# The first expert's token rows gathered as columns: products of x blocks with the place matrix, instead of a gather, a copy and a transpose

## The chip, the cores and the metric

One NeuronCore of one Trainium2 chip runs the whole kernel. The time is device time of one execution, in microseconds (us). All data are float32. Matrix products run on TensorE (PE in the profile; its weight loads are a row of their own, PEld), elementwise work on VectorE (DVE) and ScalarE (ACT), a few constants on GpSimd (POOL), and nearly all loads from HBM are issued by SyncE (SP).

## The reference, cut to what matters

One decoder layer over 256 tokens of width 1024: a mixer, then a mixture of experts. Only the second part is touched.

```python
x = x + hybrid_mixer(rmsnorm(x, g_mix), ...)
h = rmsnorm(x, g_ffn)
x = x + moe(h, ...)          # top 4 of 32 experts
out = rmsnorm(x, g_final)

# moe, per expert e, for the tokens that chose it:
logits = h @ w_router + b_router
top_v, top_i = lax.top_k(logits, 4)
gates = softmax(top_v)
gu = xb @ w_gate_up[e] + b_gate_up[e]
glu = min(gu[:, :F], 7) * sigmoid(1.702 * min(gu[:, :F], 7))
out_e = ((clip(gu[:, F:], -7, 7) + 1) * glu) @ w_down[e] + b_down[e]
```

## The kernel before

**The mixer** runs first, to about 133 us: projections, the gated linear attention, the output projection (`out_project`, L1352), all in 128x128 weight blocks.

**The experts** follow as 32 items, one for each expert, with 64 token slots each. An item's weights are six chunks of 2 MB (`gate_up` uses chunks 0 to 3, `down` chunks 4 and 5), which go through a ring of 12 slots in SBUF. SP issues the load of a chunk when the chunk that held its slot has been used (`s_used`; for the first chunk of item 0 also by quarters, `s_quarter`, and for some others by halves, `s_half`). For items 4 to 27 SP issues chunks in pairs of 4 MB (L457), when both slots of the pair are free; the first of these waits on item 2.

**An item's tokens** are found by a place matrix. `p_row[token, slot]` is 1/rms of the token where the token has this slot of the expert, else 0. `p_gate` is the same with the gate in place of 1/rms, over 128 columns. `gather` (L1389) multiplies `p_row` as 64 columns of weights with the residual stream `xs` (`x_sb` in the profile), 512 columns at a time, so that `bank[3]` holds the 64 gathered rows, one half of the width in partitions 0 to 63 and the other in 64 to 127. ACT copies this to `x_row`, TensorE transposes it in blocks of 128 (`turn_gathered`), and DVE scales it by the norm's weight into `x_t` (`keep_turned`), whose blocks `x_t[:, k, :]` are the weights in `gate_up`. For item `it + 1` this happens under the products of item `it`. For item 0 nothing lies ahead of it but the router, so it is written out by hand.

**From the residual stream to item 0**, the stretch of the change, PE's order is: the last part of `out_project`; logits of the second token tile, blocks 4 and 5 (`logits(1, 4, 6)`); the transposes of x blocks 6 and 7 (`transpose_x(1, 6, 8, 5)`, L1361), which wait for DVE's last addition to `xs` (L960); two idle products (`idle`, L1339, on constants); logits of blocks 6 and 7, which wait for DVE's copy of the transposes (L996, `s_trD`); a product that starts the second tile's ranks (L1427); the gather of tile 0; the rank product of tile 1 (L1431), which waits for DVE's choice of the experts (`chosen`, L964 to L969); the counts (L1433); one idle product; the gather of tile 1, which waits for the second `p_row` (L975); two idle products; `turn_first`: the transposes of the gathered rows in two halves (L1453), each when ACT has copied its half (L690), with an idle product between them, and then two transposes of `gates4` (L1458); then item 0's first product, which waits for DVE's first half of `x_t` (L1038, `s_xt_a`). Under the gather DVE turns the logits into gates (L1003 to L1009, with one exponential on ACT), copies them four times side by side (`gates4`, L1033), and scales the two halves of `x_t` (L1038). After them it writes item 0's `p_gate` (L1021) and waits for the transposed gates (`s_gt`), which it keeps as `gates_t` (L1044).

**Inside item 0** (`products`), PE runs chunk 0 (16 matmul records in the trace, two for each float32 product), the two transposes of `p_gate` (`turn_gates`, L1547), chunk 1, and so on. ACT's first copy into the second half of `gu_sb` waits for `s_gt`.

Of the kernel before, what the change touches and what calls it, by code (L numbers as in the profile page):

```python
# [6 lines left out]
P = 128  # L7
D = 1024
T = 256
TT = T // P  # L10
KT = D // P
# [18 lines left out]
SLOTS = 64  # L30
# [121 lines left out]
def build(nc, x, x_cols, cols_in, w_in, w_gk_down, w_gk_up, w_out, w_router, b_router, w_expert, b_gate_up, w_down_last, b_down, norm_final_g, out):  # L152
# [3 lines left out]
    ALU = mybir.AluOpType  # L156
# [8 lines left out]
    with ctx:  # L165
        def sem(name):
            return ctx.enter_context(nc.semaphore(name))
# [191 lines left out]
        s_xg = sem("x_gathered")  # L359
        s_xr_a = sem("first_x_row_half_ready")  # L360
        s_xT_a = sem("first_x_half_turned")
# [227 lines left out]
        def _(act_e):  # L589
# [97 lines left out]

            for f in range(2):
                act_e.wait_ge(s_xg, 1)
                act_e.copy(x_row[:, f * 256:(f + 1) * 256], bank[3][:, f * 256:(f + 1) * 256]).then_inc((s_xr_a, s_xr)[f], 1)  # L690
            act_e.preload_act_table_set("sigmoid_and_others")

            def keep_gathered(it):

                act_e.wait_ge(s_xg, it + 1)
                act_e.copy(x_row[:, :], bank[3][:, :]).then_inc(s_xr, 1)  # L696
# [99 lines left out]
        def _(dve):  # L796
            steps = [0]

            def link(ins):
                steps[0] += 1  # L800
                ins.then_inc(s_dve, 1)
                dve.wait_ge(s_dve, steps[0])
# [168 lines left out]
            def rank_and_place(t):  # L971
# [34 lines left out]
            link(dve.tensor_tensor(ex[:, :, :], ex[:, :, :], chosen[:, :, :], ALU.mult))  # L1006
            link(dve.tensor_reduce(ngt[:, :], ex[:, :, :], AX.X, ALU.add))
            link(dve.reciprocal(ngt[:, :], ngt[:, :]))
            dve.tensor_tensor(gates[:, :, :], ex[:, :, :],  # L1009
                              ngt[:, :].rearrange("p (t a) -> p t a", a=1).broadcast_to([P, TT, E]), ALU.mult).then_inc(s_gtk, 1)  # L1010
            dve.wait_ge(s_gtk, 1)

            def place_rows(e, slots):
# [11 lines left out]
            def keep_turned(it):  # L1025
# [8 lines left out]
                            .broadcast_to([P, TT, SPLITS, E])).then_inc(s_gtk, 1)  # L1034
            for i in range(2):
                dve.wait_ge((s_xT_a, s_xT)[i], 1)
                f = slice(2 * i, 2 * i + 2)
                dve.tensor_tensor(x_t[:, :, :].rearrange("p (a f) s -> p a f s", a=2)[:, :, f, :],  # L1038
                                  bank[(2, 4)[i]][:, 0:256].rearrange("p (f a s) -> p a f s", f=2, a=2),
                                  cols[:, COL_FFN:COL_FFN + KT].rearrange("p (a f s) -> p a f s", a=2, s=1)[:, :, f, :]  # L1040
                                  .broadcast_to([P, 2, 2, SLOTS]), ALU.mult).then_inc((s_xt_a, s_xt)[i], 1)
            place_gates(0, slot1[:, :])
# [138 lines left out]
        def _(pe):  # L1181
# [154 lines left out]
            def idle(n):  # L1336

                for _ in range(n):
                    mm(bank[1][:, 0:P], ones[:, :], before[:, :], start=True, stop=True)  # L1339
# [45 lines left out]
            def gather(ts=range(TT)):  # L1385
# [5 lines left out]
                if TT - 1 in ts:  # L1391
                    ins.then_inc(s_xg, 1)

            every = range(KT)
            out_project(0, 0, 0, every, False)
# [24 lines left out]
            pe.wait_ge(s_trA, 4)  # L1420
            logits(1, 4, 6)
            transpose_x(1, 6, 8, 5)
            idle(2)
            pe.wait_ge(s_trD, 1)
            logits(1, 6, 8)
            pe.wait_ge(s_p0, 1)
            mm(bank[5][:, E:2 * E], ones[:, :], chosen[:, 0, :], start=True, stop=False)  # L1427
            gather([0])

# [6 lines left out]
            pe.wait_ge(s_p0, 2)  # L1436
            gather([1])
            idle(2)
            nb = BLOCKS - 1

            def turn_gathered(it):

                pe.wait_ge(s_xr, it + 1)
                for f in range(4):
                    ins = nc.tensor.transpose(bank[3][:, f * P:(f + 1) * P], x_row[:, f * P:(f + 1) * P], ident[:, :])  # L1445
                ins.then_inc(s_xT, 1)

            def turn_first():

                for i in range(2):  # L1450
                    pe.wait_ge((s_xr_a, s_xr)[i], 1)
                    for f in range(2 * i, 2 * i + 2):
                        ins = nc.tensor.transpose(bank[(2, 4)[i]][:, f % 2 * P:(f % 2 + 1) * P], x_row[:, f * P:(f + 1) * P], ident[:, :])  # L1453
                    ins.then_inc((s_xT_a, s_xT)[i], 1)
                    idle(1 - i)
                pe.wait_ge(s_gtk, 2)
                for t in range(TT):
                    ins = nc.tensor.transpose(bank[6][:, t * P:(t + 1) * P],  # L1458
                                              gates4[:, t, :, :].rearrange("p a e -> p (a e)"), ident[:, :])
                ins.then_inc(s_gt, 1)  # L1460

            turn_first()

# [25 lines left out]
            def gate_up(it, j, ks):  # L1489
# [6 lines left out]
                for kk in ks:  # L1496
                    if in_pieces and kk % 2 == 0:
                        pe.wait_ge(s_piece[it, j][kk // 2], 16)
                    k = 4 * (j % 2) + kk
                    if isinstance(it, int) and it == 0 and k == 2:  # L1500
                        pe.wait_ge(s_xt, 1)
# [67 lines left out]
            def products(it, following):  # L1569
# [5 lines left out]
                gate_up(it, 0, range(4))  # L1575
                turn_gates(it)
                gate_up(it, 1, range(4))
                if known == 1:
# [180 lines left out]
```

## Time and profile before

| what | value |
|---|---|
| median of 3 runs | 1042.41 us (1041.95 to 1043.14) |
| the profiled execution, its own time | 1042.84 us |
| its span in the trace | 1041.1 us |
| PE busy | 1009.0 us (97%) |
| chain that ended last | PE 79%, DMA 19%, issue 1% |
| HBM read | 422.48 MB, 407 GB/s over the span |
| item 0's products begin | 139.95 us |

Times in the rows are microseconds from the start of the span. A float32 product shows as two weight loads and two matmuls (x2), a transpose as one of each. The ends of matmuls are modelled, so the profile's rows of PE overlap by some tenths of a microsecond, and the rows of PEld, whose starts are apart by what a load occupies, say more exactly when PE took the next piece of work.

### The profile page before, as it was taken

To read this page: it belongs to the slowest core of one execution; us is meant where nothing else is said; L and a number is where in the kernel's file an instruction comes from. 1 tells how busy PE (TensorE), PEld (TensorE's weight loads), DVE (VectorE), ACT (ScalarE), POOL (GpSimd) and SP (SyncE) were. 2 spreads that over 40 slices of the span, in tenths; PEclk is the share of its full clock that TensorE was granted. 3 is DMA by queue.
4 is the path that set the end of the run, shared out by engine and by line. 5 is a ranking of instruction groups with operands and counts; after the bars stand their busy time and mean duration, and the time that the engine had idled before them with its cause. 6 is when DMAs were issued, how large, how long until landed. Compare 5 with 4: busy or idle time off the path is not lost.

```text
span 1041.1 us, 12117 instructions
## 1 busy us (share of the span) xinstructions
PE 1009.0 (97%) x4824; PEld 412.3 (40%) x4824; DVE 245.0 (24%) x625; ACT 140.8 (14%) x281; POOL 6.5 (1%) x24
## 2 busy tenths in 40 slices
PE   8999999999999999999999999999999999999996
PEld 7688843333333333333333333333333333333333
DVE  2264132112122222222221122221212121122122
ACT  1100121111111111111111111111111111111112
POOL 1000000000000000000000000000000000000000
PEclk9999999999999999999999999999999999999999
DMA  9983789999999999999999999999999999999995
GB/s 367 408 369 134 311 343 422 387 426 423 420 435 429 429 434 429 434 429 434 429 428 436 431 433 429 429 434 429 436 428 434 429 428 436 426 427 427 426 421 222
DMA packets 23270, 423.86 MB, mean 407 GB/s; under 512 B 2888, under 2 KB 3408, under 8 KB 5840
## 3 DMA queue, kind: packets, MB, share of 16 engines
q1 hardware_dynamic: 22320, 422.45, 95.6%
q10 hardware_dynamic: 928, 1.09, 0.3%
q8 instruction: 17, 0.28, 0.1%
q14 instruction: 5, 0.04, 0.0%
HBM read 422.48 MB, written 1.05 MB: 407 GB/s over the span
## 4 chain that ended last, share of the span: by engine, by line
PE 79%; DMA 19%; issue 1%; DVE 0%; ACT 0%; SPq 0%; DVEq 0%; PEldq 0%
PE bank L1503 33%; DMA ring<-in_w_expert 19%; PE bank L1523 18%; PE bank L1243 5%; PE bank L1389 5%; PE y L1566 4%; PE bank L1541 3%; PE y L1352 2%; PE bank L1227 1%; PE bank L1445 1%; PE bank L1218 1%; PE bank L1352 1%; PE bank L1547 1%; PE bank L1624 1%; DMA h_t<-in_x_cols 1%
## 5 line engine op out<-in xcount | busy, mean ns | idle before, releaser
L1503 PE MATMUL bank<-ring,x_t 128*64 128x512 f32 x1984 | 447.1, 597 | 0.0
L1523 PE MATMUL bank<-ring,act 128*64 128x512 f32 x992 | 230.5, 596 | 14.2 <-DMA ring<-in_w_expert 14.2
L1503 PEld LDWEIGHTS bank<-ring,x_t 128*64 128x64 f32 x1984 | 133.9, 136 | 261.9 <-issue 257.1
L1523 PEld LDWEIGHTS bank<-ring,act 128*64 128x64 f32 x992 | 68.4, 137 | 145.2 <-issue 144.5
L1076 DVE TENSOR_TENSOR gu_b<-bank,bias_t 128x512 f32<-128x512 f32 x64 | 44.2, 691 | 330.3 <-PE bank L1541 330.2
L704 ACT COPY gu_sb<-bank 128x512 f32<-128x512 f32 x64 | 37.4, 585 | 222.6 <-PE bank L1503 222.6
L1566 PE MATMUL y<-z,p_t 64*128 64x512 f32 x248 | 61.6, 615 | 0.0
L1389 PE MATMUL bank<-x_sb,p_row 128*64 128x512 f32 x256 | 60.6, 593 | 0.0
L1029 DVE TENSOR_TENSOR x_t<-bank,cols 128x512 f32<-128x512 f32 x30 | 20.7, 691 | 164.9 <-PE bank L1445 164.9
L1243 PE MATMUL bank<-h_t,ring 128*128 128x256 f32 x256 | 56.1, 380 | 0.0
L1015 DVE TENSOR_SCALAR p_row<-slot,rank,rstd 128x64 f32<-128x64 f32 x62 | 16.7, 311 | 165.1 <-PE bank L1547 165.1
L708 ACT ACTIVATE act<-gu_b 128x256 f32<-128x256 f32 x62 | 25.8, 416 | 196.0 <-DVE gu_b L1082 196.0
L1243 PEld LDWEIGHTS bank<-h_t,ring 128*128 128x128 f32 x256 | 48.4, 190 | 7.0 <-issue 0.5
L1541 PEld LDWEIGHTS bank<-ident,gu_sb 128*128 128x128 f32 x256 | 26.8, 140 | 50.7 <-issue 50.2
L1541 PE MATMUL bank<-ident,gu_sb 128*128 128x128 f32 x256 | 42.0, 286 | 0.1
L700 ACT COPY p_t<-bank 128x256 f32<-128x256 f32 x31 | 11.5, 372 | 189.6 <-PE bank L1547 189.6
L1389 PEld LDWEIGHTS bank<-x_sb,p_row 128*64 128x64 f32 x256 | 18.2, 137 | 35.6 <-issue 35.4
L712 ACT COPY z<-bank 128x512 f32<-128x512 f32 x31 | 18.2, 587 | 89.3 <-PE bank L1523 89.3
L1566 PEld LDWEIGHTS y<-z,p_t 64*128 64x128 f32 x248 | 21.3, 186 | 20.0 <-issue 15.0
L1092 DVE TENSOR_TENSOR act<-act,gu_b 128x256 f32<-128x256 f32 x62 | 26.3, 425 | 6.5
L1087 DVE SCALAR_TENSOR_TENSOR gu_b<-gu_b 128x256 f32<-128x256 f32 x64 | 27.2, 425 | 2.2
L696 ACT COPY x_row<-bank 128x512 f32<-128x512 f32 x31 | 18.1, 585 | 62.8 <-PE bank L1389 62.8
(231 smaller groups left out, 403.2 us busy)
## 6 DMA issues: line engine op xcount, KB each, us to landing
ring<-in_w_expert SPq DMA_DIRECT2D x72, 4096.0 KB, 36.1
ring<-in_w_expert SPq DMA_DIRECT2D x36, 2048.0 KB, 47.4
ring<-in_w_expert SPq DMA_DIRECT2D x18, 1024.0 KB, 10.7
ring<-in_w_in SPq DMA_DIRECT2D x5, 2048.0 KB, 25.1
ring<-in_w_out SPq DMA_DIRECT2D x2, 2048.0 KB, 26.9
ring<-in_w_expert SPq DMA_DIRECT2D x4, 512.0 KB, 5.6
ring<-in_w_down_last SPq DMA_DIRECT2D x4, 512.0 KB, 25.3
ring<-in_w_down_last SPq DMA_DIRECT2D x2, 1024.0 KB, 24.6
```

The source lines that it names most:

```text
L704: act_e.copy(gu_sb[:, h, :], bank[h][:, :]).then_inc(s_guk, 1)
L708: act_e.activation(act_of(it)[:, 4 * h:4 * h + 4, :], gu_b[:, 0, :, :], ACT.Sigmoid, scale=ALPHA).then_inc(s_sig, 1)
L1076: dve.tensor_tensor(gu_b[:, :, :, :], bank[2][:, :].rearrange("p (f a s) -> p a f s", a=2, f=4), bias_t[:, :, 4 * h:4 * h + 4, ds(e, 1)] . ...
L1087: dve.scalar_tensor_tensor(out=gu_b[:, 1, :, :], in0=gu_b[:, 1, :, :], scalar=1.0, in1=gu_b[:, 0, :, :], op0=ALU.add, op1=ALU.mult).then_i ...
L1092: dve.tensor_tensor(act_of(it)[:, 4 * h:4 * h + 4, :], act_of(it)[:, 4 * h:4 * h + 4, :], gu_b[:, 1, :, :], ALU.mult).then_inc(s_av, 1)
L1243: ins = mm(dst[:, m * T:(m + 1) * T], w[:, k, (2 * i + m) * P:(2 * i + m + 1) * P], h_t[:, k, :], start=k == 0, stop=k == KT - 1)
L1352: ins = mm(dst[:, c0:c0 + 256], y_t[:, k, t * P:(t + 1) * P], w[:, k, :], start=j == 0, stop=j == KT - 1)
L1389: ins = mm(bank[3][a * SLOTS:(a + 1) * SLOTS, :], p_row[:, t, :], xs[:, t, a * HALF:(a + 1) * HALF], start=t == 0, stop=t == TT - 1)
L1503: ins = mm(bank[h][a * SLOTS:(a + 1) * SLOTS, :], x_t_of(it)[:, k, :], w[:, kk, a, :], start=k == 0, stop=k == KT - 1)
L1523: ins = mm(bank[0][a * SLOTS:(a + 1) * SLOTS, :], act_of(it)[:, k, :], w[:, kk, a, :], start=k == 0, stop=k == KT - 1)
L1541: ins = nc.tensor.transpose(bank[2][:, f * P:(f + 1) * P], gu_sb[:, h, f * P:(f + 1) * P], ident[:, :])
L1566: mm(y_ps[t][nn][:, :], p_t_of(it)[r, t * P:(t + 1) * P], z[r, :], start=first, stop=False, skip_group_check=True).then_inc(s_y, 1)
```

## The change

Item 0's rows are gathered the other way round. `gather_first` takes a 128x128 block of `xs` as the weights and `p_row` as the 64 moving columns, eight blocks for each of the two token tiles. The result is already turned: four blocks in `bank[2]`, four in `bank[3]`. So ACT's two copies to `x_row`, the four transposes behind them, and five of the six idle products go. DVE's two scalings (`keep_first`) read the two banks, blocks 0 to 3 and blocks 4 to 7, and stand further ahead in DVE's order. The eight products of tile 0 are spread over three places: two ahead of the last transposes of x, three in place of two idle products, three in place of the gather of tile 0. The two transposes of `gates4` move behind item 0's first chunk (`turn_all_gates`). Item 0 waits for the second half of `x_t` at its fourth block instead of its third.

```diff
-            for f in range(2):
-                act_e.wait_ge(s_xg, 1)
-                act_e.copy(x_row[:, f * 256:(f + 1) * 256], bank[3][:, f * 256:(f + 1) * 256]).then_inc((s_xr_a, s_xr)[f], 1)
...
             link(dve.tensor_reduce(ngt[:, :], ex[:, :, :], AX.X, ALU.add))
+
+            def keep_first(i):
+
+                dve.wait_ge((s_xT_a, s_xT)[i], 1)
+                k = slice(i * KT // 2, (i + 1) * KT // 2)
+                dve.tensor_tensor(x_t[:, k, :], bank[2 + i][:, 0:KT // 2 * SLOTS].rearrange("p (k s) -> p k s", s=SLOTS),
+                                  cols[:, COL_FFN:COL_FFN + KT].rearrange("p (k s) -> p k s", s=1)[:, k, :]
+                                  .broadcast_to([P, KT // 2, SLOTS]), ALU.mult).then_inc((s_xt_a, s_xt)[i], 1)
+
+            keep_first(0)
             link(dve.reciprocal(ngt[:, :], ngt[:, :]))
...
             dve.wait_ge(s_gtk, 1)
+            keep_first(1)
...
-            for i in range(2):
-                dve.wait_ge((s_xT_a, s_xT)[i], 1)
-                f = slice(2 * i, 2 * i + 2)
-                dve.tensor_tensor(x_t[:, :, :].rearrange("p (a f) s -> p a f s", a=2)[:, :, f, :],
...
+            def gather_first(t, k0, k1):
+
+                for k in range(k0, k1):
+                    f = k % (KT // 2)
+                    ins = mm(bank[2 + k // (KT // 2)][:, f * SLOTS:(f + 1) * SLOTS], xs[:, t, k * P:(k + 1) * P], p_row[:, t, :],
+                             start=t == 0 and f == 0, stop=t == TT - 1 and f == KT // 2 - 1, skip_group_check=True)
+                    if t == TT - 1 and f == KT // 2 - 1:
+                        ins.then_inc((s_xT_a, s_xT)[k // (KT // 2)], 1)
...
             logits(1, 4, 6)
+            pe.wait_ge(s_p0, 1)
+            gather_first(0, 0, 2)
             transpose_x(1, 6, 8, 5)
-            idle(2)
+            gather_first(0, 2, 5)
             pe.wait_ge(s_trD, 1)
             logits(1, 6, 8)
-            pe.wait_ge(s_p0, 1)
             mm(bank[5][:, E:2 * E], ones[:, :], chosen[:, 0, :], start=True, stop=False)
-            gather([0])
+            gather_first(0, 5, KT)
...
             idle(1)
             pe.wait_ge(s_p0, 2)
-            gather([1])
-            idle(2)
+            gather_first(1, 0, KT)
...
-            def turn_first():
-
-                for i in range(2):
-                    pe.wait_ge((s_xr_a, s_xr)[i], 1)
-                    for f in range(2 * i, 2 * i + 2):
-                        ins = nc.tensor.transpose(bank[(2, 4)[i]][:, f % 2 * P:(f % 2 + 1) * P], x_row[:, f * P:(f + 1) * P], ident[:, :])
-                    ins.then_inc((s_xT_a, s_xT)[i], 1)
-                    idle(1 - i)
+            def turn_all_gates():
                 pe.wait_ge(s_gtk, 2)
                 for t in range(TT):
...
-                    if isinstance(it, int) and it == 0 and k == 2:
+                    if isinstance(it, int) and it == 0 and k == 3:
                         pe.wait_ge(s_xt, 1)
...
                 turn_gates(it)
+                if known == 0:
+                    turn_all_gates()
                 gate_up(it, 1, range(4))
```

How the order of work moves is shown on two engines. On PE, from the logits of the second tile (`logits`, L1367) to the end of item 0's second chunk, the kernel before has these rows (a row's `x2` counts products here, not passes; `out<-moving,weights`):

```order
L1367 MATMUL y<-wr_g,h_t 128x32 x2
L1361 MATMUL y<-ident,x_sb 128x128 x2
L1339 MATMUL bank<-before,ones 128x128 x2
L1367 MATMUL y<-wr_g,h_t 128x32 x2
L1427 MATMUL y<-chosen,ones 128x32
L1389 MATMUL bank<-x_sb,p_row 64x512 x2
L1431 MATMUL y<-chosen,before 128x32
L1433 MATMUL y<-ones,chosen 32x1 x2
L1339 MATMUL bank<-before,ones 128x128
L1389 MATMUL bank<-x_sb,p_row 64x512 x2
L1339 MATMUL bank<-before,ones 128x128 x2
L1453 MATMUL bank<-ident,x_row 128x128 x2
```

Between the last of these and item 0's chunk 0 (L1503) stand one more idle product, the other two transposes of `x_row` and the two transposes of the gates (L1458).

The same stretch of PE in the changed kernel, where L1398 is `gather_first` and L1460 the transposes of the gates:

```order
L1367 MATMUL y<-wr_g,h_t 128x32 x2
L1398 MATMUL bank<-p_row,x_sb 128x64 x2
L1361 MATMUL y<-ident,x_sb 128x128 x2
L1398 MATMUL bank<-p_row,x_sb 128x64 x3
L1367 MATMUL y<-wr_g,h_t 128x32 x2
L1437 MATMUL y<-chosen,ones 128x32
L1398 MATMUL bank<-p_row,x_sb 128x64 x3
L1441 MATMUL y<-chosen,before 128x32
L1443 MATMUL y<-ones,chosen 32x1 x2
L1339 MATMUL bank<-before,ones 128x128
L1398 MATMUL bank<-p_row,x_sb 128x64 x8
L1503 MATMUL bank<-ring_49,x_t 64x512 x8
```

The row `x8` of L1503, item 0's chunk 0, now stands directly behind the last gather. The two transposes of the gates follow one row later, behind those of `p_gate`.

On DVE, from the end of the second `p_row` to item 0's `p_gate`, the kernel before has:

```order
L1003 TENSOR_TENSOR ex<-lg,lmax 128x64
L1006 TENSOR_TENSOR ex<-ex,chosen 128x64
L1007 TENSOR_REDUCE ngt<-ex 128x2
L1008 RECIPROCAL ngt<-ngt 128x2
L1009 TENSOR_TENSOR gates<-ex,ngt 128x64
L1033 COPY gates_63<-gates 128x256
L1038 TENSOR_TENSOR x_t<-bank,cols 128x2x128
L1038 TENSOR_TENSOR x_t<-y,cols 128x2x128
L1021 TENSOR_SCALAR p_gate<-slot_73,rank_75,gates 128x128 x2
```

The same stretch of DVE in the changed kernel, with `keep_first` as L1009 and the gates as L1015, has:

```order
L999 TENSOR_TENSOR ex<-lg,lmax 128x64
L1002 TENSOR_TENSOR ex<-ex,chosen 128x64
L1003 TENSOR_REDUCE ngt<-ex 128x2
L1009 TENSOR_TENSOR x_t<-bank,cols 128x256
L1014 RECIPROCAL ngt<-ngt 128x2
L1015 TENSOR_TENSOR gates<-ex,ngt 128x64
L1009 TENSOR_TENSOR x_t<-bank,cols 128x256
L1040 COPY gates_63<-gates 128x256
L1028 TENSOR_SCALAR p_gate<-slot_73,rank_75,gates 128x128 x2
```

The first half of `x_t` has moved ahead of the reciprocal and the gates, the second ahead of the copy of the gates.

## Rows read from the trace of the kernel before

**Rows 1.** The page, busy time of each engine (share of the span) and instructions.

```profile
PE 1009.0 (97%) x4824; PEld 412.3 (40%) x4824; DVE 245.0 (24%) x625; ACT 140.8 (14%) x281; POOL 6.5 (1%) x24
```

**Rows 2.** Chain that ended last, from 600 us: start, us, what.

```profile
683.45 3.46 PE bank L1523 x16
...
687.28 48.20 DMA ring<-in_w_expert
```

**Rows 3.** Who waited for whom: us in total, times, longest.

```profile
SPq L457 <- PE bank L1503: 397.9, 48, 10.7
...
PE bank L1523 <- DMA ring<-in_w_expert: 14.2, 8, 1.8
```

**Rows 4.** Windows: PE, PEld, DVE, ACT, POOL busy; granted clock, DMA share, GB/s.

```profile
150.00:200.00 50.00, 49.68 (x232) 16.80 (x228) 11.90 (x36) 6.14 (x12) 0.00 (x0) 1.00 1.01 424
...
204.00:205.00 1.00, 1.00 (x16) 0.53 (x16) 0.16 (x1) 0.54 (x1) 0.00 (x0) 1.00 0.08 33
...
210.00:250.00 40.00, 39.84 (x188) 13.50 (x186) 7.85 (x20) 5.14 (x10) 0.00 (x0) 1.00 1.01 427
```

**Rows 5.** Chain that ended last, from 115 to 145 us.

```profile
133.38 0.45 PE y L1361 x2
...
133.85 0.44 DVE h_t L996
...
134.34 0.65 PE y L1367 x4
...
136.33 0.41 PE y L1431 x2
...
137.37 1.08 PE bank L1389 x4
...
139.80 0.22 PE y L1458 x2
140.02 3.58 PE bank L1503 x16
143.60 0.37 PE bank L1547 x2
```

**Rows 6.** Weight loads in order of time: start, their time together, line, xcount.

```profile
127.96 0.97 PEld L1367 LDWEIGHTS y<-wr_g,h_t 128*128 128x128 f32 x8 [0.64 <-ACT h_t L661]
...
132.42 0.63 PEld L1367 LDWEIGHTS y<-wr_g,h_t 128*128 128x128 f32 x4
133.38 0.20 PEld L1361 LDWEIGHTS y<-ident,x_sb 128*128 128x128 f32 x2 [0.33 <-DVE x_sb L960]
133.55 0.53 PEld L1339 LDWEIGHTS bank<-before,ones 128*128 128x128 f32 x4
134.33 0.52 PEld L1367 LDWEIGHTS y<-wr_g,h_t 128*128 128x128 f32 x4 [0.26 <-DVE h_t L996]
134.78 0.30 PEld L1427 LDWEIGHTS y<-chosen,ones 128*128 128x128 f32 x2
135.12 0.20 PEld L1389 LDWEIGHTS bank<-x_sb,p_row 128*64 128x64 f32 x4
```

**Rows 7.** DVE in order of time, 138 to 150 us.

```profile
138.09 0.22 DVE L1007 TENSOR_REDUCE ngt<-ex 128x2 f32<-128x64 f32 x1
...
139.40 0.42 DVE L1038 TENSOR_TENSOR x_t<-bank,cols 128x256 f32<-128x256 f32 x1 [0.30 <-PE bank L1453]
...
149.90 0.69 DVE L1076 TENSOR_TENSOR gu_b<-bank,bias_t 128x512 f32<-128x512 f32 x1 [4.76 <-PE bank L1541]
```

**Rows 8.** PE in order of time, 66 to 72 us: start, time together, line, xcount.

```profile
69.71 1.56 PE L1321 MATMUL y<-q_dec,state 64*128 64x64 f32 x24
```

**Rows 9.** Weight loads in order of time, 80 to 150 us, columns as in Rows 6.

```profile
100.43 13.79 PEld L1352 LDWEIGHTS y<-ring,y_t 128*128 128x128 f32 x64
```

**Rows 10.** One window in the kernel's last microseconds, columns as in Rows 4.

```profile
1036.00:1038.00 2.00, 0.00 (x0) 0.00 (x0) 1.06 (x3) 0.86 (x1) 0.00 (x0) 0.50 0.36 132
```

**Rows 11.** The last products on PE, in order of time, 1028 to 1041 us.

```profile
1031.88 1.14 PE L1633 MATMUL y<-z,p_t_last 64*128 64x256 f32 x8 [0.56 <-ACT z L758]
```

More of the change, by code:

```diff
@@ L359, in build @@
         s_xg = sem("x_gathered")
-        s_xr_a = sem("first_x_row_half_ready")
         s_xT_a = sem("first_x_half_turned")
@@ L685, in _ @@
             act_e.activation(ex[:, :, :], ex[:, :, :], ACT.Exp).then_inc(s_le, 1)
-            for f in range(2):
-                act_e.wait_ge(s_xg, 1)
-                act_e.copy(x_row[:, f * 256:(f + 1) * 256], bank[3][:, f * 256:(f + 1) * 256]).then_inc((s_xr_a, s_xr)[f], 1)
             act_e.preload_act_table_set("sigmoid_and_others")
             def keep_gathered(it):
-                act_e.wait_ge(s_xg, it + 1)
+                act_e.wait_ge(s_xg, it)
                 act_e.copy(x_row[:, :], bank[3][:, :]).then_inc(s_xr, 1)
@@ L1034, in _ @@
                             .broadcast_to([P, TT, SPLITS, E])).then_inc(s_gtk, 1)
-            for i in range(2):
-                dve.wait_ge((s_xT_a, s_xT)[i], 1)
-                f = slice(2 * i, 2 * i + 2)
-                dve.tensor_tensor(x_t[:, :, :].rearrange("p (a f) s -> p a f s", a=2)[:, :, f, :],
-                                  bank[(2, 4)[i]][:, 0:256].rearrange("p (f a s) -> p a f s", f=2, a=2),
-                                  cols[:, COL_FFN:COL_FFN + KT].rearrange("p (a f s) -> p a f s", a=2, s=1)[:, :, f, :]
-                                  .broadcast_to([P, 2, 2, SLOTS]), ALU.mult).then_inc((s_xt_a, s_xt)[i], 1)
             place_gates(0, slot1[:, :])
@@ L1436, in _ @@
             pe.wait_ge(s_p0, 2)
-            gather([1])
-            idle(2)
+            gather_first(1, 0, KT)
             nb = BLOCKS - 1
             def turn_gathered(it):
-                pe.wait_ge(s_xr, it + 1)
+                pe.wait_ge(s_xr, it)
                 for f in range(4):
@@ L1460, in turn_first @@
                 ins.then_inc(s_gt, 1)
-            turn_first()
             def count_extras():
```

## The prediction, made before the changed kernel ran

> **What bounds the kernel now.** I read the page first: PE is busy 97% of the span [rows 1]. That is a busy share, not yet a bound, so the chain of waits comes next. From item 0 to 687 us the chain is PE's own work without a break. Then it turns: a chunk pair comes free, SP issues its load at once, the load lands 48.20 us later and PE waited for it [rows 2]. The list of waits says the same: SP waited 48 times on products, 397.9 us in all, and PE waited 8 times for weights, 14.2 us in all [rows 3]. So late in the loop the weight stream ends last; it moves some 430 GB/s without a pause.
>
> What starts that stream? The windows show the DMA engines full from 150 to 200 us, all but empty at 204 to 205 us (share 0.08), and full again from 210 us [rows 4]. At 204 us they wait for PE: the first pair load of the loop needs two chunks of item 2 to be used. PE itself is never late there (busy 49.68 of 50 us). The stream therefore starts at a moment that PE sets, with nothing left over from before. A microsecond that PE gains or loses before item 0 reaches 204 us whole, and from there the end, one for one. Thus the sum is made on PE's path from 132 to 144 us.
>
> In that stretch the chain is [rows 5]: DVE's last addition to x, two transposes of it, DVE's copy (over at 134.29), the logits, DVE's choice, the rank product at 136.33, the second gather at 137.37, then ACT's copy, the transposes, the gates' transposes, and item 0's 16 matmuls, over at 143.60.
>
> **The price of one new product.** It has 128x128 weights and 64 moving columns, in two passes. No row has exactly this. Two rows bracket it: logits (32 moving columns) and idle products (128 moving columns). Eight loads of the first take 0.97 us with the last alone 0.19, so (0.97 - 0.19)/7 = 0.111 us apart; four of the second (0.53 - 0.19)/3 = 0.113 [rows 6]. Narrower and wider cost the same, so the load sets the pace and 64 columns should too: 0.222 us a product. The far bounds are 0.13 (24 passes of 64x64 in 1.56 us [rows 8], half the rows, half the columns) and 0.43 (64 loads at 256 columns in 13.79 us [rows 9]). I take 0.222.
>
> The Trainium skill ("TensorE: Matmul & The Clock Gate", Back-to-back issue gap) gives about 81 ns for each matmul in a sustained stream of load and matmul at 128 columns, which would be 0.16 us a product. The rows here have 0.111 us a pass where it has 0.081. By the page the eight last products would take 1.30 us instead of 1.78 and the gain would be some 0.4 us larger; the sum goes by the rows.
>
> **Part by part.**
>
> 1. *Two products ahead of the last transposes.* The loads of the logits begin at 132.42 and take 0.63 us, the last of them 0.19, so the next could begin at 132.42 + 0.63 - 0.19 + 0.11 = 132.97. DVE releases the transposes at 133.38. The four new loads take 132.97 to 133.41 [rows 6]. The gap holds them but for 0.03 us; since the matmuls behind them have to drain too, I take a delay of 0.05 (0 to 0.2). Everything on the chain down to the second gather shifts with it. `p_row` of tile 0, for which they wait, is long there. If the products cost more, there is no cover here: each 0.1 us a product is 0.2 us.
>
> 2. *Three products for two idle ones.* Six loads, 0.67 us, from 133.60 end at 134.27; DVE's copy ends at 134.29 + 0.05. Cost 0, with 0.07 us to spare; at a higher price the logits wait.
>
> 3. *Three products for the gather of tile 0.* The old gather ran 1.08 us from 135.12, hidden ahead of the rank product at 136.33 [rows 5]. The new ones load from about 135.06 to 135.72 and end near 136.0. Hidden, 0.3 us to spare.
>
> 4. *Tile 1.* Begins at 137.37 + 0.05 = 137.42. Sixteen loads, 0.111 apart: the last begins at 139.09. Meanwhile the first half: its last load begins at 138.20, its product ends 0.3 later (logits: last load 134.66, end 134.99), 138.5; DVE is free since 138.31 + 0.05 [rows 7]; scaling 0.42 us, and some 0.1 to wake PE: 139.05. So the first half of `x_t` is ready just before PE has finished the second half of the gather, and PE binds, by 0.1 to 0.2 us. Item 0's first load follows the last one by 0.11 or, as 64-column loads behind 128-column ones do (134.89 to 135.12 [rows 6]), by 0.23: 139.32. Before, it was 139.95. So chunk 0 starts and ends 0.63 us earlier. The second half of `x_t` is scaled behind the gates by about 139.95, and is needed at the fourth block, 6 x 0.224 us after 139.32, which is 140.66: hidden, 0.7 to spare.
>
> 5. *Out of the way:* ACT's copies, four transposes, three idle products, the gates' transposes and their waits are what made up 138.45 to 139.95 [rows 5, 6]; they are replaced, not added, and already counted in 4. ACT's table load moves ahead and nobody waits for it.
>
> 6. *The gates' transposes behind chunk 0.* On the chain the two took 0.22 us before item 0 [rows 5]; now they take 0.22 us behind `p_gate`'s. Their gates are ready by about 140.3, chunk 0 ends near 143.0. What waits behind them: chunk 1, 0.22 us later; on DVE the copy of the gates, the counts and item 1's places, some 2 us of work from about 143.6, when its next work that is waited for begins at 149.90 [rows 7]; on ACT the second half of gate and up, some 10 us later. All hidden.
>
> 7. *SP.* No issue moves in its order. The quarters of chunk 0 come free 0.6 us earlier, while the DMA engines have some slack; that fills a gap that 204 us forgets anyway.
>
> **Sum:** +0.05 (already in the 0.63) - 0.63 + 0.22 = -0.41 us at chunk 1, and the same at the end. The profiled execution, 1042.84 us, would become 1042.43; the median of the runs shown is 0.43 below it, 1042.41, so about **1042.0 us**.
>
> About 0.2% (2.1 us) is what a measurement of this kernel can tell from no change, and the three runs shown are themselves 1.2 us apart. The forecast is inside that.
>
> **The rivals.**
>
> *The new products cost 0.43 us each (slower).* A float32 weight load from `xs` behind narrow products could run at the pace of the wide ones [rows 9]. Then parts 1 and 2 delay the logits by 0.42 + 0.6 = 1.0, tile 1 takes 3.4 us instead of 1.78, and item 0 begins near 141.9: +1.9, plus 0.22, gives 1044.5. It turns from gain to loss at (13 products on the path, 0.41 us to lose) 0.222 + 0.03 = 0.25 us a product. Against it: both rows of Rows 6 with 0.11 us a pass. For it: the turning point is near.
>
> *The clock falls (slower).* Idle products and wide gathers are replaced by narrow products. The one low window is in the last microseconds, 0.50 from 1036 us on [rows 10], after PE had stopped at 1033.02 [rows 11]. Against it: PE stands still for 3 us there and nowhere here, and the change opens no new gap on it. If half the clock held for some 4 us of item 0, it would cost 2 us: 1044.0.
>
> *No effect at the end.* If the stream were bound before 204 us, the gain would be lost: 1042.4. Against it: the empty window [rows 4].
>
> *The first half of `x_t` binds after all.* If its semaphore and DVE's read of PSUM take 0.3 us more than in part 4, PE waits for it: gain 0.2, 1042.2. That margin is only 0.1 to 0.2 us.
>
> *Cheaper products (faster).* At 0.13 [rows 8] tile 1's products take 1.0 us, and DVE's first scaling binds: free at 138.36, done at 138.8, PE at 138.9. Item 0 begins 1.05 us earlier, less 0.22: gain 0.8, 1041.6. (The page's 0.16 us, above, would fall under this rival.)
>
> **Chances.** Forecast (gain 0.3 to 0.6) 0.54; the half of `x_t` binds 0.08; no effect 0.12; cheaper products 0.12; dearer products 0.06; clock 0.04; something unseen, either side, 0.04. The range has to hold the middle cases and the scatter of a median of a few such runs (those shown lie 0.5 below and 0.7 above theirs), and reaches some way to the dear ones: 1040.9 to 1043.5. By more than 0.2%: faster 0.03, slower 0.05, within 0.92.
>
> **What would show it.** PE's loads of L1398 0.111 us apart; the last transposes of x (L1361) at 133.38 to 133.5; the second `p_row` at most 0.1 later; item 0's first load at 139.2 to 139.5; `p_gate`'s transposes 0.6 and chunk 1 0.4 earlier; the first pair load of the loop at 204.2 instead of 204.6. It would be wrong if L1398's loads stand further apart than 0.125, if PE waits for `x_t`, if the windows from 132 to 150 show a clock below 1.00, or if the 0.4 us at 204 us is not there at 687 us.

## The result: slower by 2.5 us, because TensorE's clock falls to half ahead of item 0 and in it

The changed kernel took 1045.28 us (median of 16 runs, 1044.15 to 1046.13) against 1042.78 us of the kernel before (16 runs, 1041.95 to 1043.37). The ratio is 1.0023, with a 95% interval of 1.0016 to 1.0029. The forecast was 1042.0 us, with a range up to 1043.5. The profiled execution took 1044.50 us, span 1042.7 us (before: 1042.84 and 1041.1). One more execution of the kernel before, beside the first experiments, was in a slow state at 2673.49 us and is left out of every count below.

The first place to look is item 0's chunk 0, since the forecast's sum ends there. This is the chain of waits of the changed kernel from 115 to 145 us (start, us, what), to be read against [rows 5]:

```profile
132.58 0.36 PE y L1367 x4
132.95 0.47 PE bank L1398 x4
133.42 0.23 PE y L1361 x2
133.65 0.62 PE bank L1398 x6
134.26 0.55 PE y L1367 x4
...
136.16 0.41 PE y L1441 x2
...
137.20 2.37 PE bank L1398 x16
139.57 4.84 PE bank L1503 x16
144.41 0.37 PE bank L1547 x2
144.78 0.22 PE y L1460 x2
```

L1398 is `gather_first`. Up to 137.20 all went by the forecast. Then the 16 matmuls of tile 1's gather take 2.37 us, where they take 2.00 in the same code with the clock kept (e6 below), and the same 16 matmuls of chunk 0 that took 3.58 us before take 4.84. Nothing waits there. The windows of the same kernel say why (us, then PE, PEld, DVE, ACT, POOL busy; **granted clock**, DMA share, GB/s):

```profile
130.00:136.00 6.00, 5.71 (x41) 5.20 (x40) 2.31 (x11) 1.38 (x5) 0.00 (x0) 1.00 0.61 224
136.00:137.00 1.00, 0.84 (x8) 0.79 (x8) 0.46 (x3) 0.00 (x0) 0.00 (x0) 1.00 1.20 492
137.00:138.00 1.00, 1.00 (x9) 0.81 (x9) 0.59 (x4) 0.62 (x2) 0.00 (x0) 1.00 1.15 492
138.00:139.00 1.00, 1.00 (x10) 1.00 (x9) 0.69 (x4) 0.92 (x1) 0.00 (x0) 0.83 0.69 295
139.00:140.00 1.00, 1.00 (x5) 0.67 (x6) 0.49 (x2) 0.00 (x0) 0.00 (x0) 0.50 1.22 524
140.00:141.00 1.00, 1.00 (x4) 0.24 (x2) 0.81 (x4) 0.00 (x0) 0.00 (x0) 0.50 1.07 459
141.00:142.00 1.00, 1.00 (x4) 0.24 (x2) 0.00 (x0) 0.00 (x0) 0.00 (x0) 0.50 0.22 82
142.00:143.00 1.00, 1.00 (x8) 0.32 (x6) 0.00 (x0) 0.00 (x0) 0.00 (x0) 0.96 0.64 66
```

The granted clock is 1.00 until 138.7, 0.50 (1.2 of 2.4 GHz) until 142.1, then 1.00 again. PE is busy the whole time that it is low, with half as many matmuls in a window (x4 for x8). Before the change it was 1.00 from the first product to the last, and PE was no busier ahead of 138 us than after it. Windows of the kernel before:

```profile
130.00:136.00 6.00, 5.71 (x34) 4.33 (x33) 2.17 (x10) 1.38 (x5) 0.00 (x0) 1.00 0.63 229
136.00:137.00 1.00, 0.87 (x9) 0.62 (x8) 0.43 (x3) 0.00 (x0) 0.00 (x0) 1.00 1.29 541
```

From 130 to 138 us PE stands idle for 0.42 us in the kernel before and for 0.45 in the changed one. What differs is what it does: the windows count 49 matmuls before and 58 after. The mean granted clock shows it in every run: 0.994 to 0.996 in all 16 runs of the changed kernel, 0.997 or 0.998 in the kernel before, where only the end, after PE's last product [rows 10, 11], is low.

The page after, to [rows 1]: PE has ten matmuls more (32 for 16 new products, less 8 of the old gather, 10 of idle products and 4 transposes), and 1.7 us more busy time, about what the stretch at half clock adds (0.37 and 1.26 us):

```profile
PE 1010.7 (97%) x4834; PEld 414.7 (40%) x4834; DVE 244.8 (23%) x625; ACT 140.2 (13%) x279; POOL 6.5 (1%) x24
```

### The profile page after: what moved, and what is told of

It reads as the page before. It is cut to its first block, busy times and chain, and to the rows that moved or that the text cites. A ratio compares the mean times of both kernels' runs of the same rounds, so it can differ in the third digit from the quotient of the medians.

```text
span 1042.7 us, 12111 instructions
## 1 busy us (share of the span) xinstructions
PE 1010.7 (97%) x4834; PEld 414.7 (40%) x4834; DVE 244.8 (23%) x625; ACT 140.2 (13%) x279; POOL 6.5 (1%) x24
## 4 chain that ended last, share of the span: by engine, by line
PE 75%; DMA 23%; issue 1%; DVE 0%; ACT 0%; SPq 0%; DVEq 0%; PEldq 0%
PE bank L1503 30%; DMA ring<-in_w_expert 23%; PE bank L1523 18%; PE bank L1243 5%; PE bank L1389 4%; PE y L1566 4%; PE bank L1541 3%; PE y L1352 2%; PE bank L1227 1%; PE bank L1454 1%; PE bank L1218 1%; PE bank L1352 1%; PE bank L1547 1%; PE bank L1626 1%; DMA h_t<-in_x_cols 1%
## 5 line engine op out<-in xcount | busy, mean ns | idle before, releaser
L1503 PE MATMUL bank<-ring,x_t 128*64 128x512 f32 x1984 | 448.3, 598 | 0.0
L1503 PEld LDWEIGHTS bank<-ring,x_t 128*64 128x64 f32 x1984 | 134.2, 137 | 262.8 <-issue 257.9
L1389 PE MATMUL bank<-x_sb,p_row 128*64 128x512 f32 x248 | 58.5, 592 | 0.0
```

What stands on the lines that cost most here:

```text
L1389: ins = mm(bank[3][a * SLOTS:(a + 1) * SLOTS, :], p_row[:, t, :], xs[:, t, a * HALF:(a + 1) * HALF], start=t == 0, stop=t == TT - 1)
L1503: ins = mm(bank[h][a * SLOTS:(a + 1) * SLOTS, :], x_t_of(it)[:, k, :], w[:, kk, a, :], start=k == 0, stop=k == KT - 1)
```

## The experiments

Two theories stood at the start. **The clock:** with the new gather PE has less of the work that keeps the clock up, and the loss is the spell at half clock. **The rival:** the loss comes from the order (the gates' transposes behind chunk 0, DVE's copies ahead), and the clock is a side show.

The kernels ran in three sets (e1 to e4, e5 to e8, e9 to e12), each on one chip with the kernel before (medians 1042.96, 1042.97 and 1043.10 us). To compare profiles, I count from the end of the output projection in the chain (132.81 us in the kernel before), which executions reach up to 0.6 us apart.

| kernel | median against before, us | ratio, 95% interval | runs with mean clock 0.996 or less | to chunk 0, us | to chunk 1, us |
|---|---|---|---|---|---|
| before | | | 0 of 94 | 7.21 | 11.16 |
| changed | +2.50 | 1.0016 to 1.0029 | 16 of 16 | 6.99 | 12.42 |
| e1_gates_only | +0.06 | 0.9992 to 1.0010 | 0 of 11 | 7.06 | 11.30 |
| e2_wide_fill | +0.07 | 0.9992 to 1.0010 | 0 of 11 | 7.19 | 11.36 |
| e3_128_columns | -0.37 | 0.9988 to 1.0005 | 0 of 11 | 6.71 | 10.88 |
| e4_no_idle | -0.07 | 0.9999 to 1.0016 | 4 of 12 | 7.07 | 11.09 |
| e5_changed_again | +2.00 | 1.0009 to 1.0027 | 10 of 11 | 8.50 | 13.67 |
| e6_two_idle_back | -0.54 | 0.9985 to 1.0004 | 0 of 11 | 6.62 | 10.79 |
| e7_gates_ahead | +3.83 | 1.0025 to 1.0052 | 5 of 5 | 8.60 | 14.63 |
| e8_128_tile0 | -0.46 | 0.9994 to 1.0012 | 3 of 11 | 6.66 | 10.83 |
| e9_128_tile1 | +1.00 | 1.0001 to 1.0019 | 6 of 11 | 7.93 | 12.10 |
| e10_128_and_idle | -0.49 | 0.9987 to 1.0005 | 0 of 11 | 6.71 | 10.88 |
| e11_idle_gates_ahead | +0.82 | 1.0000 to 1.0019 | 2 of 11 | 7.83 | 11.78 |
| e12_two_idle_again | -0.87 | 0.9984 to 1.0002 | 0 of 11 | 6.61 | 10.78 |

The last two columns are of the profiled execution alone, the others of all runs. Where a kernel keeps its clock in one run and loses it in another, the profile shows one case only: one that kept it in e4, e8 and e11, one that lost it in e5 and e9. The interval goes by the means of the runs, so the few long runs of e4 and e8 lift it above what the median says. The mean clock of a run is rounded to 0.001, which is some 2 us at half clock, so a spell of up to about 2 us can hide in a 0.997: the counts of runs that fell are lower bounds.

### One part alone: the gates' transposes

```diff
--- before
+            def turn_all_gates():      # the last lines of turn_first, now a function of their own
...
                 turn_gates(it)
+                if known == 0:
+                    turn_all_gates()
                 gate_up(it, 1, range(4))
```

> The kernel before with one part of the change alone: the two transposes of the gates stand behind item 0's first chunk. Theory (the loss is the clock that falls to half at 138.7 us, and narrow products in the gather bring it): here the gather is the old one, so the granted clock stays 1.00 from 130 to 150 us, item 0 starts 0.2 us earlier and its second chunk at the same time; the median is that of the kernel before within 0.3 us. Rival (what is put behind the first chunk makes the wait, on DVE or ACT): the loss of some 2 us appears here too.

Measured: 1043.02 against 1042.96 us, with the clock at 1.00 from 130 to 150 us in the profile. On the old gather this part costs nothing, so the rival falls as far as one part alone can show it (with the new gather: e7 and e11). It gains nothing either, since chunk 0 now waits for DVE's first half of `x_t` where it stood behind the transposes.

### More columns in PE's gaps

```diff
--- changed
             gather_first(0, 5, KT)
+            wide(1)        # ones x xs[:, 0, 0:512] into bank[1]
...
-            idle(1)
+            wide(1)
```

> The changed kernel with one product of 512 moving columns in the gap ahead of the rank product of tile 1, and another in place of the idle product of 128 columns behind the counts. Both should fit into time in which PE waits for DVE (0.58 us and 0.42 us). Theory (what PE streamed ahead of 138.7 us lets the clock fall): with more columns streamed the granted clock stays 1.00, chunk 0 takes 3.6 instead of 4.84 us, and the median comes to 0.4 us below the kernel before. Rival (the clock falls whatever fills the gaps, or the loss has another source): 1045 us again.

Measured: 1043.03 against 1042.96 us; the clock is 1.00 in the windows from 130 to 150 us and chunk 0 takes 3.58 us. The clock theory holds, but the gain is gone too. The chain of this kernel (L1406 is the wide product, L1447 the rank product):

```profile
136.20 0.91 PE bank L1406 x2
137.12 0.14 PE y L1447 x2
...
137.47 1.06 PE bank L1406 x2
138.53 1.73 PE bank L1398 x16
140.26 3.58 PE bank L1509 x16
```

The two did not fit into the gaps; they hold 0.91 and 1.06 us of the chain, and tile 1's gather starts 5.46 us behind the output projection, against 4.62 in e6 below. My expectation had them fit into waits of 0.58 and 0.42 us.

### 128 moving columns instead of 64

The cut is shortened; DVE's scaling, not shown, reads the first 64 of every 128 columns.

```diff
--- changed
-   mm(bank[..][:, f * SLOTS:(f + 1) * SLOTS], xs[..], p_row[:, t, :], ...)
+   mm(bank[..][:, f * P:(f + 1) * P], xs[..],
+      p_row[:, t, :].rearrange("p (a s) -> p a s", a=1).broadcast_to([P, 2, SLOTS]), ...)
```

> The changed kernel with each gathering product streaming its 64 place columns twice, so 128 moving columns; the second copy goes to columns of PSUM that nobody reads. The weight loads set the pace (0.111 us a pass at 32 and at 128 columns), so PE's times should not change. Theory (narrow products bring the clock down): the clock stays at 1.00 or falls for less, and the median is 1042.4 to 1043.5. Rival (not the columns but the weight loads, the order or the gap ahead of the rank product): the clock falls as before, 1045 us.

Measured: 1042.59 against 1042.96 us, mean clock 0.997 or 0.998 in all 11 runs. The same number of products in the same order, the same wait of 0.58 us ahead of the rank product, and little time added (chunk 0 at 6.71 us, against 6.62 in e6):

```profile
137.84 2.05 PE bank L1398 x16
139.89 3.58 PE bank L1504 x16
```

Tile 1's products take 2.05 us here and 2.00 in e6 with 64 columns. So the order of the work, the weight loads and the wait are not enough to let the clock fall. How wide the products are makes the difference, for 0.09 us.

### The kernel before without its idle products

```diff
--- before
-            idle(2)        # and idle(1), idle(2), idle(1 - i): six products in all
```

> The kernel before without its six idle products (L1339), all else as it was. If idle products hold the clock up in this stretch, it falls to half between 135 and 143 us here too, although the wide gathers are there: +1.5 to +2.5 us. If the wide gathers are enough, the clock stays 1.00 and the median is 0 to 0.5 us below that of the kernel before.

Measured: a median of 1042.89 us, but in two groups. Eight of 12 runs took 1041.76 to 1043.67 us at a mean clock of 0.997 or 0.998, and four took 1043.91 to 1046.15 at 0.994 or 0.995. Neither expectation is met alone. The wide gathers mostly hold the clock by themselves, but not always, and with the idle products the kernel before never lost it in 94 runs. So they were not filler that could go for free, which is how the forecast counted them. The profile caught a run that held the clock, with PE idle for longer than in the changed kernel:

```profile
130.00:136.00 6.00, 5.26 (x31) 4.02 (x30) 1.96 (x8) 1.38 (x5) 0.00 (x0) 1.00 0.63 231
136.00:138.00 2.00, 1.45 (x10) 0.69 (x10) 1.08 (x6) 0.25 (x1) 0.00 (x0) 1.00 1.13 471
```

That is 1.29 us of idle time in 8, against 0.45 in the changed kernel, which lost the clock in 26 of its 27 runs (the first 16 and e5). PE's idle time alone does not decide it.

### The changed kernel again, profiled in its slower group

> The changed kernel once more, beside the next three on one chip. Its 16 runs so far lie in two groups: 1044.2 to 1044.5 with a mean granted clock of 0.996, and 1044.9 to 1046.1 with 0.994. Theory: in the first the half clock holds once for 3.4 us from about 138.7, in the second for about twice that, which (1 - 0.994) - (1 - 0.996) of 1043 us at half clock, 4 us, would be. A profile from the second group would show the low clock reach to 145 us and item 0's second chunk slowed too. Rival: the second group has its low clock elsewhere, or the weight stream takes longer there.

Measured: 1044.97 us. Six of the 11 runs are at 0.994, two at 0.995, two at 0.996 (1043.16 and 1044.10) and one at 0.998 (1043.24). The profile fell into the slower group. Windows of it, columns as above:

```profile
136.00:136.50 0.50, 0.12 (x2) 0.00 (x0) 0.44 (x3) 0.00 (x0) 0.00 (x0) 1.00 1.12 475
136.50:137.00 0.50, 0.44 (x2) 0.44 (x2) 0.01 (x1) 0.00 (x0) 0.00 (x0) 0.64 1.15 475
137.00:137.50 0.50, 0.50 (x6) 0.42 (x6) 0.28 (x2) 0.00 (x0) 0.00 (x0) 0.50 0.94 377
...
143.00:143.50 0.50, 0.50 (x4) 0.24 (x2) 0.00 (x0) 0.00 (x0) 0.00 (x0) 0.53 0.08 33
143.50:144.00 0.50, 0.50 (x4) 0.14 (x2) 0.00 (x0) 0.00 (x0) 0.00 (x0) 1.00 0.00 0
```

and its chain:

```profile
138.18 3.31 PE bank L1398 x16
141.49 4.58 PE bank L1503 x16
146.07 0.37 PE bank L1547 x2
```

The half clock lasts from 136.6 to 143.5, some 6.8 us where the other profile has 3.4. It slows tile 1's gather (3.31 for 2.00 us) and chunk 0 (4.58 for 3.58). Chunk 1 begins 2.5 us later than in the kernel before, where the other profile lost 1.26. That the two groups of times are these two lengths is what the two profiles and the mean clocks fit; my expectation put the second spell's end at 145 us, 1.5 too late, and chunk 1 was not slowed.

### Two idle products back

```diff
--- changed
             gather_first(0, 5, KT)
+            idle(2)
 
             pe.wait_ge(s_cho, 2)
```

> The changed kernel with two idle products of 128 columns in the gap ahead of the rank product of tile 1, where PE waited 0.58 us. If the clock falls because PE stood still there, it stays at 1.00 now and the median is 0.3 us below the kernel before. If what counts is how much PE streams over the whole stretch, 512 columns are a small part and the clock falls as before in most runs: 1044 to 1046 us.

Measured: 1042.43 against 1042.97 us, clock 0.997 or 0.998 in all 11 runs. That is the first case of the expectation: the wait is filled and the clock stays. It does not prove that the wait was the cause, since the two products also add columns, and since e3 holds the clock with the wait left as it was. The chain:

```profile
135.50 0.70 PE bank L1398 x6
136.19 0.50 PE bank L1339 x4
136.69 0.35 PE y L1442 x2
...
137.68 2.00 PE bank L1398 x16
139.68 3.58 PE bank L1504 x16
...
143.85 5.30 PE bank L1504 x24
```

The idle products fill the time in which PE waited for DVE's choice, and the rank product starts 3.63 us behind the output projection, 0.06 later than in e5.

> The changed kernel with two idle products back in the gap, a second time, to see its gain over the kernel before on one more set of runs: 0.4 us by the prediction's sum (the first set gave 0.54), with the clock at 1.00 in every run until PE stops.

Measured on a second set of runs: 1042.23 against 1043.10 us, clock 0.997 or 0.998 in all 11. Twice the changed kernel with two more idle products is ahead of the kernel before, by 0.54 and 0.87 us, each time with an interval that still includes 1.

### The gates ahead of item 0, at the low and at the full clock

```diff
--- changed (e7), and with idle(2) back (e11)
+            turn_all_gates()
...
-                if known == 0:
-                    turn_all_gates()
```

> The changed kernel with the other part undone: the gates' transposes stand ahead of item 0 again. By the theory (the narrow products bring the clock down) it loses as the changed kernel does: 1044 to 1046 us, mean granted clock 0.994 to 0.996. Rival (the second part of the change is the cause): 1042.6.

Measured: 1046.80 us, 3.83 over the kernel before, all five runs at 0.993 to 0.995. The loss is there without the second part of the change, as the theory has it, and is larger by 1.8 us than in e5. In the two profiles chunk 1 is 0.96 us later (14.63 against 13.67). The full clock shows where that comes from:

> The two idle products back, and the gates' transposes ahead of item 0 again: what the second part of the change is worth at the full clock. DVE now scales both halves of x_t ahead of the copy of the gates, so PE waits for the gates until about 140.4 us and item 0's second chunk comes some 0.7 us later than with the gates behind: 1043.1 against 1042.4 us. Rival: if the clock fell here, 1045 us and more.

Measured: 1043.92 against 1043.10 us. The clock held in the profile and in 9 of 11 runs; two fell (0.996 and 0.994). The chain of e11:

```profile
137.71 2.01 PE bank L1398 x16
...
139.81 0.42 DVE x_t L1009
140.24 0.21 DVE gates L1040
...
140.49 0.44 PE y L1461 x2
140.93 3.58 PE bank L1506 x16
```

PE ends its gather at 139.72 and then waits 0.77 us, because DVE copies the gates only behind both halves of `x_t`. Chunk 1 begins 11.78 us behind the output projection, against 10.78 with the gates behind chunk 0 (e12). So the move that was worth nothing on the old gather (e1) is worth 1.0 us at chunk 1 on the new one, with DVE's work in the new order. I had expected 0.7. The medians are further apart, 1.69 us (1.3 with the two fallen runs of e11 left out); what the rest is stays open.

### Where the columns have to be

> The changed kernel with 128 moving columns in the eight products of tile 0 alone, 64 in those of tile 1. The clock fell at 138.7 us, in the middle of tile 1's products. If what PE did ahead of 137 us decides, this holds the clock: 1042.6 us. If the products of tile 1 count alike, it holds in some runs and falls in others: two groups of times, a median between 1042.6 and 1045.

Measured: 1042.51 against 1042.97 us. The clock held in 8 of 11 runs (1041.99 to 1043.08 us) and fell in three (1043.97 to 1046.08): the second case of the expectation, with the median just under it. Eight products widened by 64 columns stream more than the two idle products of 128 in e6, and yet the clock falls in some runs here and in none of 22 there. So the number of columns alone does not put these kernels in order either; e6 also filled the wait, and e8 leaves it.

> The changed kernel with 128 moving columns in the eight products of tile 1 alone. With the 128 columns in tile 0 alone the clock held in 8 of 11 runs. The profiles of the changed kernel show it fall at 137.3 and at 138.7 us, in or ahead of tile 1's products, so widening these comes late: I expect the clock to fall in half of the runs or more, and a median of 1043 to 1045 us. If it holds in all runs, what runs in tile 1's own time is enough.

Measured: 1044.10 against 1043.10 us, six of 11 runs at 0.996 or less, as expected. Three more, at 0.997, took 1043.78 to 1044.18 us, more than any run of e3, e10 or e12, so they may have had a short spell. The profile shows the clock fall in the same place as in e5 (136.6 us there, not the 137.3 of my expectation), ahead of tile 1's products, and come back sooner:

```profile
136.00:138.00 2.00, 1.56 (x11) 1.42 (x11) 1.08 (x6) 0.26 (x1) 0.00 (x0) 0.70 1.09 459
138.00:139.00 1.00, 1.00 (x6) 1.00 (x6) 0.45 (x2) 0.99 (x1) 0.00 (x0) 0.50 1.07 459
139.00:140.00 1.00, 1.00 (x7) 1.00 (x6) 0.23 (x1) 0.29 (x1) 0.00 (x0) 0.50 0.80 344
140.00:141.00 1.00, 1.00 (x9) 0.88 (x10) 0.50 (x4) 0.00 (x0) 0.00 (x0) 0.89 1.15 492
```

Widening one tile lowers the number of runs that lose the clock, from 26 of 27 to 3 of 11 (tile 0) or at least 6 of 11 (tile 1); with both widened none of 11 did.

> The changed kernel with both remedies: 128 moving columns in all 16 gathering products and two idle products in the gap ahead of the rank product. Both lie in time that PE has. The clock should stay 1.00 in every run, and the median be 0.4 us below that of the kernel before, as the sum of the prediction has it; no better than with either alone.

Measured: 1042.61 against 1043.10 us, mean clock 0.997 or 0.998 in all 11 runs. As expected, both remedies together gain no more than one.

## Why the prediction was wrong, step by step

**The step that failed is the rival "The clock falls".** It was named, but it got a chance of 0.04, and the range was closed below it. The argument was that PE stands still for 3 us before the one low window [rows 10, 11], and that the change opens no such gap. That takes one fall, after a stop, as the only way in which the clock falls. It is also not quite so that the change opens no gap: tile 0's wide gather had filled PE to 0.13 us before the rank product, and its narrow products leave the wait of 0.58 us in the second row here (0.44 us by the matmuls):

```profile
134.83 0.75 PEld L1398 LDWEIGHTS bank<-p_row,x_sb 128*128 128x128 f32 x6
136.16 0.30 PEld L1441 LDWEIGHTS y<-chosen,before 128*128 128x128 f32 x2 [0.58 <-DVE chosen L965]
```

But nothing there is like the 3 us stop. The clock falls with PE busy 5.71 of 6.00 us (130 to 136), as in the kernel before, and with no wait longer than this one. The prediction had itself named a clock below 1.00 between 132 and 150 us as a sign of being wrong, and that sign came.

The price was the smaller part of it. The 2 us lie between what the clock cost at chunk 1 in the two profiles, against e6: 1.63 us (12.42 - 10.79) and 2.88 (13.67 - 10.79). In the medians it cost more, 2.5 to 3.0 us: the changed kernel is 2.00 and 2.50 us behind the kernel before, and e6 0.54 ahead of it. So even its 1044.0 us was 1.3 too low.

What was missing is the reverse question: what did the things that go do there? Six idle products on constants stood in exactly this stretch, and the change takes five of them. The forecast counted them only as time that PE gets back (parts 2 and 5), not as work that might hold the clock. e4 shows that they do, in 4 of 12 runs, and e6 that two of them, put back where PE waits, are enough. From the logits on, PE's rows around them are products of 1 to 128 moving columns; the two gathers of 512 columns were the wide ones, and they went in the same change. e3 shows that this counts: with 128 columns for 64 and nothing else changed on PE, none of 11 runs fell.

The Trainium skill ("TensorE: Matmul & The Clock Gate", Why this matters for your kernels) puts throughput drops in the middle of a kernel down to idle gaps between bursts of matmuls, and asks to keep TensorE continuously busy. In this case's trace the only wait of note ahead of the fall was 0.58 us, PE's idle time from 130 to 138 us was within 0.03 us of what it was before the change, and e4 mostly held the clock with more of it. The measurement decides: a PE that the profile shows as busy is no guarantee.

**The sum itself held**, where the clock does. e6 and e12 are the changed kernel with its clock kept:

- *Price of a product.* 0.222 us from the bracket of two rows. In the changed kernel's loads ahead of the fall (first row above) six take 0.75 us, the last of them 0.19, so they are 0.112 us apart. Widening to 128 columns (e3) left the loads as far apart, as the bracket said. The Trainium skill ("TensorE: Matmul & The Clock Gate", Back-to-back issue gap) has about 81 ns for each matmul in a sustained stream; this case's rows do not show it. So the rivals of dearer and of cheaper products are out.
- *Part 1, two products ahead of the last transposes: +0.05.* From DVE's last addition to its copy of the transposes it was 0.95 us (132.90 to 133.85), after it 0.99 (132.69 to 133.68): +0.04. *Parts 2 and 3: hidden.* The rank product comes 3.43 us behind that addition before and 3.47 after; nothing was added.
- *Part 4: chunk 0 earlier by 0.63.* 7.21 - 6.62 = 0.59 (e6). PE did bind, not DVE's half of `x_t`, which in e6 was done at 139.31 us, 0.3 ahead of chunk 0's first load.
- *Part 6: +0.22.* The two transposes take 0.22 us of the chain in every kernel that has them there. Nothing waited behind them. But the part was costed as an exchange of 0.22 for 0.22. Its worth is 1.0 us at chunk 1 (e11 against e12), since with the new gather and DVE's new order the gates are the last thing ready; "ready by about 140.3" stood in the text without the conclusion.
- *Sum: -0.41 at chunk 1.* 11.16 - 10.79 = 0.37 (e6), 0.38 (e12).
- *The starting point* was low by luck of the draw: the three runs shown had a median of 1042.41 us, the 16 runs 1042.78. By the same sum from there the forecast would be 1042.4.

**From chunk 1 to the end, one for one: right to 687 us in most profiles, loose by half a microsecond at the end.** The changed kernel comes to the table products at 205.44 us instead of 204.41 (+1.03), behind which the loop's first pair is loaded:

```profile
201.86 3.58 PE bank L1503 x16
205.44 0.38 PE bank L1474 x12
...
688.77 48.27 DMA ring<-in_w_expert
```

At the pair that binds late in the loop it is 1.49 us later (688.77 against 687.28 [rows 2]). So 0.46 us came in between. In e6 it is 0.69 (0.12 us ahead of the kernel before at chunk 1, 0.57 behind at this load) and in e9 0.41. In these three a further load, begun at 632.8 to 634.0 us, is on the chain. The other profiles carry their shift from chunk 1 to this load within 0.02 us, e11 within 0.1: counted from the start of the trace, e10 has -0.15 and -0.16 us, e12 -0.17 and -0.17, e5 +2.69 and +2.68, e7 +3.66 and +3.65. Behind it up to 0.6 us are added or lost; e5's span ends 2.1 us later, not 2.7. The shift at chunk 1, counted from the output projection, and that of the median agree to about 0.5 us: +2.51 and +2.00 (e5), +3.47 and +3.83 (e7), +0.62 and +0.82 (e11), -0.37 and -0.54 (e6), -0.38 and -0.87 (e12). (The changed kernel's first profile is of its faster group: +1.26 at chunk 1 and +1.66 in its own time, where the median has +2.50.) The rival "no effect at the end" is out for losses. For a gain the traces of e10 and e12 speak against it (spans 0.5 and 0.6 us shorter), but the profiled execution of e6 took 1043.49 us, more than the kernel before.

**What stays open:** what exactly the chip weighs when it grants the clock. The runs show which kernels keep it, not the quantity. The wait ahead of the rank product and the width of the products both seem to count: widening with the wait left (e3) keeps the clock, and so does filling the wait with the gather left narrow (e6, e12). No run fills the wait without adding columns, so the two are not told apart in e6. And whether the 0.4 us of gain is real: e3, e6, e10 and e12 are all ahead of the kernel before, by 0.37 to 0.87 us, but each interval includes 1.

## What to carry to other kernels

Before idle-looking products on constants are removed, or wide products replaced by narrow ones, ask for the granted clock of that stretch, and read it again afterwards; a chain that is right to 0.05 us is worth nothing if the clock halves under it. If it falls, first widen what is bound by its weight load anyway (the broadcast operand cost 0.09 us here), or put two idle products where the engine waits. And cost a moved step in the new order, not the old: the same move was worth 0 on the old gather and 1.0 us at chunk 1 on the new one.

## What was not expected of the hardware

- The granted clock fell to 0.50 with PE never waiting longer than 0.58 us ahead of it, and with PE as busy from 130 to 138 us (7.55 of 8.00) as in the kernel that never lost it (7.58). In the two profiles of the same code it stayed there from 138.7 to 142.1 and from 136.6 to 143.5.
- It is not all or nothing: the same kernel lost the clock in 3 of 11 (e8), 4 of 12 (e4), 6 of 11 (e9) or 2 of 11 runs (e11). One profile at 1.00 does not show that a kernel keeps it; the mean clock of many runs says more, down to spells of about 2 us.
- The two weight loads of a float32 product with 128x128 weights are 0.111 to 0.113 us apart with 32, 64 or 128 moving columns, which is 0.22 us a product in all three cases.
